# A two-block network on one core: order of the last split tile, of the first projections, and unread products in TensorE's waits

## What is computed

```python
def first_block(x, mem, ...):                      # 2 layers, 4 ffns
    for layer in range(2):
        x = layer_norm(ALPHA * x + 0.5 * swiglu(x, w_gu, w_down), g, b)
        o_tok, q_mem = mla_mix(...) if layer == 0 else nsa_mix(...)
        mix = concatenate([o_tok, memory_attention(q_mem, mem, w_mem_kv)]) @ w_out
        x = layer_norm(ALPHA * x + mix, g, b)
        x = layer_norm(ALPHA * x + 0.5 * swiglu(x, w_gu2, w_down2), g, b)
    return x

def second_block(x, c, ...):
    for i in range(2):
        sh1, sc1, g1, sh2, sc2, g2 = split(silu(c) @ w_ada[i] + b_ada[i], 6)
        h = rms_norm(x) * (1 + sc1) + sh1
        x = x + g1 * (hgrn2_mixer(h) if i == 0 else rglru_mixer(h))
        h = rms_norm(x) * (1 + sc2) + sh2
        x = x + g2 * peer_ffn(h)                   # 16384 experts, top 16 of 8 heads
    return rms_norm(x)
```

## Time and profile before

| | us |
|---|---|
| median of the runs | 3106.61 (3103.76 to 3108.07) |
| profiled execution | 3109.25 |
| its span, first to last instruction | 3107.6 |
| TensorE matmul busy | 3009.4 (97%) |
| TensorE weight load busy | 2668.5 (86%) |
| VectorE busy | 2322.3 (75%) |
| ScalarE busy | 1529.4 (49%) |
| GpSimd busy | 114.8 (4%) |
| mean granted TensorE clock | 0.988 |

### The profile page before, as it was taken

How to read it: one execution, slowest core, us unless ns; L and a number is a source line. 1 busy time by engine, 2 the same in 40 slices (tenths; PEclk the granted TensorE clock), 3 DMA queues, 4 the chain that set the end, 5 groups by cost and what they waited for, 6 DMA issues and landing times.

```text
span 3107.6 us, 52364 instructions
## 1 busy us (share of the span) xinstructions
PE 3009.4 (97%) x18414; PEld 2668.5 (86%) x18414; DVE 2322.3 (75%) x4339; ACT 1529.4 (49%) x2659; POOL 114.8 (4%) x132
## 2 busy tenths in 40 slices
PE   8998999999999998899999999999999999999998
PEld 7876887888578897799999988887789999988887
DVE  7856897786576787689899955555579989965555
ACT  5435543543454464555544444544645544445544
POOL 0010121001010000000000000000100000000000
PEclk9999999999999999999999999999999999999999
DMA  8762776876135542145544455555335544455554
GB/s 323 287 260 82 256 299 238 295 286 223 55 122 190 177 166 105 45 167 189 183 144 142 141 182 194 191 195 192 133 136 183 187 154 141 141 176 193 192 195 150
DMA packets 124976, 567.82 MB, mean 183 GB/s; under 512 B 13872, under 2 KB 14000, under 8 KB 97328
## 3 DMA queue, kind: packets, MB, share of 16 engines
q1 hardware_dynamic: 108864, 504.41, 46.7%
q0 software_dynamic: 15264, 58.73, 5.5%
q10 hardware_dynamic: 720, 3.00, 0.2%
HBM read 565.03 MB, written 1.05 MB: 182 GB/s over the span
## 4 chain that ended last, share of the span: by engine, by line
PE 86%; DVE 5%; ACT 2%; issue 1%; DMA 0%; DVEq 0%; ACTq 0%
PE turn L359 46%; PE gather L359 39%; ACT arena L1365 1%; PE turn L872 0%; DVE arena L2616 0%; ACT hT L1365 0%; ACT L1365 0%; DVE arena L2307 0%; DVE arena L2475 0%; DVE arena L2302 0%; DVE ring_low L2156 0%; PE gather L667 0%; DVE ring_low L2149 0%; DVE arena L2063 0%; DVE arena L2424 0%
## 5 line engine op out<-in xcount | busy, mean ns | idle before, releaser
L1365 ACT ACTIVATE dense<-ring 128x1024 fp32r<-128x1024 f32 x544 | 575.9, 1059 | 385.3 <-PE gather L359 347.8
L2638 DVE TENSOR_TENSOR ring_low<-ring,dense 128x1024 fp32r<-128x1024 f32 x544 | 662.4, 1219 | 67.8 <-ACT dense L1365 64.8
L359 PE MATMUL turn<-expert_src_high,ring_low 128*128 128x256 f32 x2496 | 698.8, 280 | 0.0
L359 PE MATMUL turn<-expert_src_high,dense 128*128 128x256 f32 x2304 | 657.8, 286 | 1.0 <-DVE expert_src_low L2140 1.0
L359 PE MATMUL turn<-expert_src_low,dense 128*128 128x256 f32 x2304 | 645.7, 280 | 0.0
L359 PE MATMUL gather<-dense 128*128 128x512 f32 x2048 | 631.6, 389 | 2.1 <-DVE ring_low L2638 2.1
L359 PE MATMUL turn<-rounded 128*128 128x512 f32 x1408 | 494.0, 392 | 0.0
L359 PEld LDWEIGHTS turn<-expert_src_high,ring_low 128*128 128x128 f32 x2496 | 471.8, 189 | 0.0
L359 PEld LDWEIGHTS gather<-dense 128*128 128x128 f32 x2048 | 384.5, 188 | 82.7 <-DVE ring_low L2638 2.9
L359 PEld LDWEIGHTS turn<-expert_src_high,dense 128*128 128x128 f32 x2304 | 435.4, 189 | 1.7 <-issue 1.7
L359 PEld LDWEIGHTS turn<-expert_src_low,dense 128*128 128x128 f32 x2304 | 435.5, 189 | 0.0
(11 more groups left out here) (259 smaller groups left out, 3888.3 us busy)
## 6 DMA issues: line engine op xcount, KB each, us to landing
ring<-tiles_in SPq DMA_DIRECT2D x544, 512.0 KB, 3.3
ring<-stream SPq DMA_DIRECT2D x205, 1024.0 KB, 5.5
arena<-ada_in POOLq DMA_DIRECT2D x96, 512.0 KB, 4.6
arena<-tables_in POOLq DMA_DIRECT2D x6, 1024.0 KB, 7.1
arena<-keys_in SPq DMA_DIRECT2D x2, 1024.0 KB, 7.8
arena<-c_in POOLq DMA_DIRECT2D x3, 512.0 KB, 5.5
hT<-x_in SPq DMA_DIRECT2D x1, 1024.0 KB, 5.3
x_rows<-rows_in ACTq DMA_DIRECT2D x1, 1024.0 KB, 21.3
```

Source lines behind the costliest of these rows:

```text
L359: return nc.tensor.matmul(out, lhsT, rhs, start=start, stop=stop, skip_group_check=True)
L1365: return nc.scalar.activation(out, in_, func, **kw)
L2638: V.tensor_tensor(tile_words(t, ring_low).bitcast(R32), tile_words(t), tile_high[:, t % AHEAD, :], ALU.subtract).then_inc(S("tile_low"), 1)
```

## The change

In the ffns' `down_last` the first three ends run through banks (0, 0) and (0, 1), then the fourth end through both, then banks (1, 0) and (1, 1) as before; likewise the experts' with their last tile. `split_mm` is made of `low_mm` and `pair_mm`; in `up_first`, ffn0 takes all paired products and then all low ones, the other ffns all low products (each waiting for the high source only) and then all paired ones. `spread_gates` uses transposes of the broadcast column. `keep_going` issues products whose result nobody reads, into a bank that is free then: seven of hT at the start, FILLERS[e] before the transposes of tt = 0 and tt = 1 of each turn, 13 in hgrn at li = 0, 24 before its gate rows, 7 and 14 around those of lru. They are identity x identity in float32, hT at the start, and one-pass products of hidden tiles for e = 2. On VectorE, the first four half heads' reciprocal of hgrn's end is taken head by head, each followed by its products.

```diff
--- before.py
+++ after.py
@@ -368,14 +368,21 @@
                 return v[:, 0:shape[0] * shape[1]].rearrange("p (a b) -> p a b", b=shape[1])
             return v[:, 0:math.prod(shape)].rearrange("p (a b c) -> p a b c", b=shape[1], c=shape[2])
+        def low_mm(bank, q, b, k, start, stop):
+            wl = ring_low[:, q % SLOTS, b * HALF + k * P:b * HALF + (k + 1) * P].bitcast(R32)
+            return mm(bank[:, 0:T], wl, src_high[:, k, :].bitcast(R32), start, stop)
+        def pair_mm(bank, i, b, k, start, stop):
+            wh = w_high[:, 2 * (i % 2) + b, k * P:(k + 1) * P].bitcast(R32)
+            return mm(bank[:, :].rearrange("p (a t) -> p a t", t=T), wh, src[:, :, k, :].bitcast(R32), start, stop)
         def split_mm(bank, q, i, b, k):
-            wh = w_high[:, 2 * (i % 2) + b, k * P:(k + 1) * P].bitcast(R32)
-            wl = ring_low[:, q % SLOTS, b * HALF + k * P:b * HALF + (k + 1) * P].bitcast(R32)
-            mm(bank[:, 0:T], wl, src_high[:, k, :].bitcast(R32), k == 0, False)
-            return mm(bank[:, :].rearrange("p (a t) -> p a t", t=T), wh, src[:, :, k, :].bitcast(R32), False, k == KC - 1)
+            low_mm(bank, q, b, k, k == 0, False)
+            return pair_mm(bank, i, b, k, False, k == KC - 1)
         def split_half(name, i, b, memory):
             return memory[:, (piece_base(name) + i) % SLOTS, b * HALF:(b + 1) * HALF]
@@ -437,6 +444,7 @@
             bank = B[3] if tt == 1 and k < 2 else Y[2 * tt + k // 4]
             return bank[:, k % 4 * P:(k % 4 + 1) * P]
+        FILLERS = [(0, 11), (0, 8), (0, 8), (0, 8), (0, 8), (31, 3), (6, 11), (5, 11), (3, 11)]
         TURN_ENDS = [(0, 3), (0, 7), (1, 1), (1, 3), (1, 7)]
         def turn_count(e, tt, k):
@@ -658,9 +666,21 @@
         @block.tensor
         def _(pe):
+            def keep_going(bank, products, left=identity, right=identity):
+                for _ in range(products):
+                    mm(bank[:, 0:P], left, right, True, True)
             def turn_rows(e):
+                before = FILLERS[e]
                 for tt in range(TT):
+                    if e == 2:
+                        keep_going(B[2], before[tt], hid_high[:, 0, 0:P].bitcast(R32), hid_high[:, 1, 0:P].bitcast(R32))
+                    else:
+                        keep_going(B[2], before[tt])
                     for k in range(KC):
                         if k % 4 == 0:
                             pe.wait_ge(S("normed"), 4 * e + 2 * tt + k // 4 + 1)
@@ -681,8 +701,8 @@
                 at = 48 * (r // 2) + 24 * (r % 2) + 16
                 for k in range(KC):
-                    last = mm(B[k // 4][:, k % 4 * P:(k % 4 + 1) * P], mod[:, at + k:at + k + 1].to_broadcast([P, P]),
-                              identity, True, True)
+                    last = nc.tensor.transpose(B[k // 4][:, k % 4 * P:(k % 4 + 1) * P],
+                                               mod[:, at + k:at + k + 1].to_broadcast([P, P]), identity)
                 last.then_inc(S("gates_spread"), 1)
             def ffn(m):
@@ -706,12 +726,37 @@
                 def up_first():
+                    def rest(f, k, first):
+                        return low_mm(B[f], q0, f, k, first and k == 0, not first and k == KC - 1)
+                    def both(f, k, first):
+                        return pair_mm(B[f], 0, f, k, first and k == 0, not first and k == KC - 1)
+                    if m == 0:
+                        pe.wait_ge(S("source_ready"), KC)
+                        for f in range(2):
+                            pe.wait_ge(S("high_ready"), w0 + f + 1)
+                            for k in range(KC):
+                                both(f, k, True)
+                        for f in range(2):
+                            half(0, f, 0)
+                            for k in range(KC):
+                                last = rest(f, k, False)
+                            last.then_inc(*((S("half_used"), 1) if f == 0 else (piece_done, 1)))
+                        return
                     for f in range(2):
                         half(0, f, 0)
                     for k in range(KC):
+                        pe.wait_ge(S("source_high"), KC * m + k + 1)
+                        for f in range(2):
+                            rest(f, k, True)
+                    for k in range(KC):
                         pe.wait_ge(S("source_ready"), KC * m + k + 1)
                         for f in range(2):
-                            last = split_mm(B[f], q0, 0, f, k)
+                            last = both(f, k, False)
                             if k == KC - 1:
                                 last.then_inc(*((S("half_used"), 1) if f == 0 else (piece_done, 1)))
@@ -738,19 +783,35 @@
                 def down_last():
-                    for tt in range(TT):
-                        for b in range(2):
-                            for i, n, tile in ((31, 2, t0 + 18), (32, 0, t0 + 20)):
-                                for j in range(2):
-                                    if tt == 0 and b == 0:
-                                        pe.wait_ge(S("hidden_ready"), tile + j + 1)
-                                        half(i, j, 0)
-                                    down_mm(i, n, j, tt, b, True)
-                                    last = down_mm(i, n, j, tt, b, False)
-                                    if tt == 1 and b == 1:
-                                        last.then_inc(*((S("half_used"), 1) if j == 0 else (piece_done, 1)))
-                            if 2 * tt + b < 3:
-                                last.then_inc(S("bank_summed"), 1)
+                    ends = [(31, 2, t0 + 18, j) for j in range(2)] + [(32, 0, t0 + 20, j) for j in range(2)]
+                    def passes(end, tt, b):
+                        i, n, _, j = end
+                        down_mm(i, n, j, tt, b, True)
+                        return down_mm(i, n, j, tt, b, False)
+                    def given(end):
+                        i, _, tile, j = end
+                        pe.wait_ge(S("hidden_ready"), tile + j + 1)
+                        half(i, j, 0)
+                    for b in range(2):
+                        for end in ends[:3]:
+                            if b == 0:
+                                given(end)
+                            passes(end, 0, b)
+                    given(ends[3])
+                    for b in range(2):
+                        passes(ends[3], 0, b).then_inc(S("bank_summed"), 1)
+                    for b in range(2):
+                        for end in ends:
+                            last = passes(end, 1, b)
+                            if b == 1:
+                                last.then_inc(*((S("half_used"), 1) if end[3] == 0 else (piece_done, 1)))
+                        if b == 0:
+                            last.then_inc(S("bank_summed"), 1)
                 up_first()
                 up(1, 1)
@@ -1066,6 +1127,7 @@
                         last = project_pair(q0 + 12 + li, Y[i], hT)
                     last.then_inc(piece_done, 1)
                     if li == 0:
+                        keep_going(Y[3], 13)
                         pe.wait_ge(S("hg_taken"), 12)
                     pe.wait_ge(S("hg_factors"), min(li, 6) + 1)
@@ -1102,6 +1164,7 @@
                     last = mm(Y[b4][:, :], mean_mat, hg_far[:, 4 * b4:4 * b4 + 4, :].rearrange("p a t -> p (a t)"),
                               True, True)
                     last.then_inc(S("hg_o_sums"), 1)
+                keep_going(B[0], 24)
                 spread_gates(0)
                 def sums_read(n):
@@ -1188,9 +1251,11 @@
                 gates(3)
                 late(1)
                 late(2)
+                keep_going(Y[3], 7)
                 pe.wait_ge(S("lru_late_taken"), 3)
                 pe.wait_ge(S("lru_taken"), 5 + 32)
                 spread_gates(2)
+                keep_going(B[2], 14)
                 out_by_source("lru_out", lru_out, lru_low,
                               lambda k: pe.wait_ge(*((S("lru_mixed"), 1) if k < 2 else (S("out_low"), KC + k - 1))),
                               native=2)
@@ -1273,17 +1338,25 @@
                 def down_last():
-                    for tt in range(TT):
-                        for b in range(2):
-                            for n in range(NKEYS - 3, NKEYS):
-                                if tt == 0 and b == 0:
-                                    down_ready(n)
-                                down_mm(n, tt, b, True)
-                                last = down_mm(n, tt, b, False)
-                                if tt == 1 and b == 1:
-                                    last.then_inc(tile_done, 1)
-                            if 2 * tt + b < 3:
-                                last.then_inc(S("rows_summed"), 1)
+                    def passes(n, tt, b):
+                        down_mm(n, tt, b, True)
+                        return down_mm(n, tt, b, False)
+                    for b in range(2):
```

(28 more changed lines are left out.)

## The result

The changed kernel takes 3084.2 us (median of 6 runs) against 3106.2 us for the kernel before (6 runs); ratio 0.9934, 95% interval 0.9923 to 0.9946. That is 22.0 us less. The profiled execution has a span of 3083.1 us against 3107.6, 24.5 less; forecast were 23.4 less, and 3083.2 us.

A forecast was written before the change was run, and what follows sets the result against it. TensorE's stream of products was taken as the bound, losing time to waits and low clock. Terms 3.3 + 8.3 - 0.1 + 13.9 + 0.2 + 0.4 = 26.0, minus 2.6, gave 23.4 less: 3083.2 us, range 3077 to 3092.

The forecast's parts named there:

- Start: Kernel start, ffn0: paired products first and seven early products of hT let TensorE start earlier; 3.3 us less (2.4 to 3.9).
- VectorE's cap: Kernel start: VectorE waits for the first ada tile until 18.84, then takes 5.5 us steps; TensorE can gain at most 3.9.
- Bank order: Ends of ffns and expert layers: taking the last split tile last covers the ring_low stalls; 8.3 us less (6 to 9).
- Source order: First projections, ffn1 to ffn3: ffn1 0.4 to 0.9 us later, ffn2 0, ffn3 0.3 earlier; together +0.1 (-0.3 to +2).
- Fillers and clock: Unread products in waits at norms, hgrn and lru remove the low-clock stretch behind each, at seven places; 13.9 us less.
- The deduction of 2.6: Taken from the 26.0 sum: clock lost again in two of five places where transposes and a wait follow fillers, 1.3 us each.
- the five: Places where transposes and a 1 to 2 us wait follow fillers: norms 1 and 4, rms before hgrn, before both experts.
- the first rival: Transposes do not hold the clock, so it is lost after them in all five places; 18 less, 3088.6 us; chance 0.25.
- clock lost in all five: Rival: clock lost after the transposes behind the fillers in all five places; 18 less, 3088.6 us; chance 0.25.
- fillers do not hold: Sign that the prediction is wrong: the clock falls right after the fillers; no size or chance of its own given.
- Gate rows: Gate rows by transposes: nothing at hgrn and lru, 0.1 us behind each expert gate; 0.2 less (0 to 2).
- Reciprocal: End of hgrn: head 0 at the same time, head 1's low part 2.2 us later; output still 0.4 earlier (-0.5 to +1.7).

## Why the prediction was right, and where not

**Start: right in size, wrong in its parts.** 3.9 gained, 3.3 taken from 2.4 to 3.9. The order alone reaches VectorE's cap; the early clock adds nothing. The first product at 9.72 and the unchanged 5.5 us steps are as forecast.

**Bank order: right, term by term.** 2.96, 1.62, 1.65, 0.38, 0.79, 1.33 against 2.9, 1.6, 1.6, 0.3, 0.7, 1.2; the old order takes all of it back.

**Source order: right in ffn1, against the kernel before.** 0.74 lost in 0.4 to 0.9; the sum had counted with the lower end, 0.4. Against the old order at the same clock the loss is twice that, 1.5; the low stretch that the kernel before has there (331.1) hid the rest. In ffn3 0.05 came of the 0.3.

**Fillers and clock: right at six of seven places** (1.54, 2.82, 1.45, 1.67, 1.64, 2.50 against 1.5, 2.8, 1.4, 1.7, 1.7, 2.4). Before hgrn it came to 0.81 of 2.4. The deduction of 2.6 for transposes and a wait behind the fillers stood for exactly this: 1.6 were lost, in one place of the five and not in two. Over the eight profiles with as many fillers, seven lost the clock again in one or two of the five: four before hgrn, three in ffn3's first piece (0.3 to 0.4 us each), two of these three also in ffn1's (1.4). Of the two causes that the prediction named together, one falls: transposes hold the clock. What the low stretches follow is waiting behind them (1.9 us before hgrn), and not every time; that part is argued from where they lie, and one profile supports it. The argument against the first rival, that norms 2 and 3 kept the clock through waits of 2.1 us, does not bear weight: without fillers both lose it, the first of them behind the same 2.12 us. The rival "clock lost in all five" still falls, and so does "fillers do not hold": without them 13.2 us go.

**Gate rows: not seen.** Of the 0.2 nothing can be told from drift, as the run with products shows.

**Reciprocal: right in its steps, too small in its harm.** Head 1's low part was forecast at 1292.9 less the shift of 14.5, 1278.4; it came at 1278.50. The output took the full 1.5 us of harm, not 1.25, so 0.04 was left of 0.4. The waits behind head 0 and head 1 are 0.57 and 0.33 us for the 0.7 and 0.6 forecast; a further 0.58 lies ahead of head 0, and the variant with the whole reciprocal has one of 0.6 there too, so it is not the edit's.

**What the prediction left out.** The attentions. It counted ten low stretches in the kernel before, and one more at 1242; the trace has two further ones ahead of the last product, at 331.1 (ffn1) and this, the joint longest, in the second attention:

```profile
798.80:809.00 10.20, 10.20 (x25) 5.85 (x24) 2.05 (x5) 1.36 (x5) 0.00 (x0) 0.50 0.01 2
```

In the changed kernel two of 3.4 us stand in its place. No part of the change touches the attentions and their waits of 1 to 2 us; their clock came out 2.06 worse in the first and 1.48 better in the second. The two nearly cancel; the first alone would have been the largest miss of all steps. Over the other profiles with fillers the second gives 1.5 or 3.2 to 3.4, and the first takes between nothing and 12 us, so this is luck of the execution. The steps sum to 26.0 in the forecast before its deduction; measured they give 25.0 without the attentions, and 24.5 with them; that total and its deduction were right for partly wrong reasons.

## What to carry to other kernels

Where TensorE's stream stops for 1 to 3 us and the stretch behind it is full of products, unread work in the wait gave back about half the length of each low stretch here, and transposes served as well as products. Fill the last wait before the dense work too, not only the first; here that rests on one profile. Where low stretches come and go between executions, judge an edit by what its own step gains and not by the total. Before splitting a step by parts to start sooner, ask which engine frees its input: the reciprocal by heads and the source order both ended an idle time that cost nothing and put a later one in its place.

## What the runs showed of the hardware

- Transposes on TensorE keep the granted clock at 1.00 as products do: 22 records before a wait of 0.6 us, clock 1.00 behind it; with nothing in the wait of 3.0 us 0.50. Whether transposes alone bring a low clock up was not tested.
- The same wait of 2.12 us between like work was followed by a granted clock of 1.00 in one execution (kernel before, norm behind ffn1) and of 0.50 in another (without fillers).
- The clock can stay at 0.50 through 37.5 us in which TensorE is busy throughout by the trace (37.50 of 37.50), in an attention of short transposes and products. At the low level work takes about twice as long (eight transposes 1.97 us against 1.03), so the busy share there says nothing of the work done.
- While GpSimd adds rows (2.4 to 3.4 us each) VectorE's cast of 128x256 took 2.38 us instead of the 0.29 of the next one and a low part 2.74 instead of 1.22. The Trainium skill ("SBUF — State Buffer", SBUF: two separate sides) has the two engines share a port that one holds for a whole instruction. The rows agree: the cast starts 0.24 us behind GpSimd's second addition and ends 0.15 us behind its end. But no run here moved GpSimd's additions.
